# Reordered start, mLSTM stage and last stage of a one-core hybrid attention and mLSTM step

## What is computed

```python
mod = jax.nn.silu(c) @ w_ada + b_ada                       # 2048 x 6144
shift, scale, gate = jnp.split(mod[:, None, :], 3, axis=-1)
h = rmsnorm(x, norm_pre) * (1 + scale) + shift
u = h @ w_in                                               # 2048 x 13320
q_a, k_a, v_a, z_a, q_m, k_m, v_m, o_m, z_m, i_m, f_m, g_a, g_m = split_in(u)
att = attend(...)                                          # differential attention, 8 heads
y_a = (rmsnorm(att) * (1 - lam_init) * silu(z_a)) @ w_br_a
hm, C1, n1, m1 = mlstm(qm, km, vm, ig, lf, C0, n0, m0)     # 4 heads
y_m = (sigmoid(o_m) * rmsnorm(hm) * silu(z_m)) @ w_br_m
y = (sigmoid(g_a) * y_a + sigmoid(g_m) * y_m) @ w_out
out = x + gate * rmsnorm(y, norm_post)
```

## Time and profile before

| | |
|---|---|
| median of 3 runs | 1985.6 us (1985.49 to 1986.94) |
| the profiled execution | 1986.92 us, span 1985.4 us |
| TensorE busy | 1936.4 us, 98% of the span |
| VectorE, ScalarE, GpSimd busy | 781.6, 642.0, 188.5 us |
| mean granted TensorE clock | 0.995 of full |
| HBM | 220.93 MB read, 17.73 MB written, 121 GB/s mean |

### The profile page before, as it was taken

How to read it: one execution, slowest core, us unless ns; L and a number is a source line. 1 busy time by engine, 2 the same in 40 slices (tenths; PEclk the granted TensorE clock), 3 DMA queues, 4 the chain that set the end, 5 groups by cost and what they waited for, 6 DMA issues and landing times.

```text
span 1985.4 us, 31138 instructions
## 1 busy us (share of the span) xinstructions
PE 1936.4 (98%) x12223; PEld 1662.7 (84%) x12223; DVE 781.6 (39%) x1666; ACT 642.0 (32%) x1144; POOL 188.5 (9%) x316
## 2 busy tenths in 40 slices
PE   5999999999999999999999999999999999999997
PEld 4778898988899998888899988878878878878885
DVE  4555234246653334454355322232232232353224
ACT  4212222235545454343333222212222222332232
POOL 2221011000020101122230000000000000010001
PEclk9999999999999999999999999999999999999998
DMA  9986663231234542223332332232232232353223
GB/s 308 311 277 191 197 221 95 78 109 49 59 109 149 175 139 71 74 77 111 101 118 84 85 85 80 83 105 80 80 104 85 80 104 81 122 188 101 80 84 117
DMA packets 165938, 240.50 MB, mean 121 GB/s; under 512 B 15065, under 2 KB 113497, under 8 KB 164073
## 3 DMA queue, kind: packets, MB, share of 16 engines
q1 hardware_dynamic: 150304, 194.03, 31.9%
q0 software_dynamic: 13264, 44.50, 6.8%
q10 hardware_dynamic: 2242, 0.19, 0.1%
HBM read 220.93 MB, written 17.73 MB: 120 GB/s over the span
## 4 chain that ended last, share of the span: by engine, by line
PE 74%; DVE 1%; POOL 1%; issue 1%; ACT 1%; DMA 0%; ACTq 0%; POOLq 0%
PE gemm L544 59%; PE bank_s L544 9%; PE bank_o L544 2%; PE bank_a L544 2%; PE bank_s L787 1%; DVE g_m L2022 1%; PE bank_a L733 0%; PE bank_s L952 0%; PE bank_s L1064 0%; POOL hm_sq L2317 0%; POOL hm_sq L2318 0%; POOL rinv L2372 0%; ACT hm_sq L1141 0%; DVE y_tok L2102 0%; PE bank_s L573 0%
## 5 line engine op out<-in xcount | busy, mean ns | idle before, releaser
L544 PE MATMUL gemm<-h_hi,w_hi 128*128 128x288 f32 (+1 forms) x2560 | 663.0, 324 | 8.1 <-DVE q_acc L1582 4.0
L1506 DVE TENSOR_TENSOR w_lo<-w_raw,w_hi 128x512 fp32r<-128x512 f32 x512 | 357.5, 699 | 782.2 <-ACT w_hi L1141 781.6
L1141 ACT ACTIVATE w_hi<-w_raw 128x512 fp32r<-128x512 f32 x512 | 322.3, 630 | 1025.1 <-PE bank_s L544 568.7
L544 PE MATMUL gemm<-h_hi,w_lo 128*128 128x288 f32 (+1 forms) x2560 | 639.2, 315 | 0.0
L544 PE MATMUL gemm<-h_lo,w_hi 128*128 128x288 f32 (+1 forms) x2560 | 638.4, 315 | 0.0
L544 PEld LDWEIGHTS gemm<-h_hi,w_hi 128*128 128x128 f32 x2560 | 425.6, 189 | 85.9 <-issue 49.0
L544 PEld LDWEIGHTS gemm<-h_lo,w_hi 128*128 128x128 f32 x2560 | 426.0, 189 | 21.1
L544 PEld LDWEIGHTS gemm<-h_hi,w_lo 128*128 128x128 f32 x2560 | 426.3, 189 | 20.3
L544 PE MATMUL gemm<-w_hi,y_all 128*128 128x512 f32 x512 | 158.8, 391 | 0.5 <-DVE g_m L2022 0.5
L544 PEld LDWEIGHTS gemm<-w_hi,y_all 128*128 128x128 f32 x512 | 95.6, 188 | 24.9 <-DVE g_m L2022 1.4
L544 PE MATMUL gemm<-w_lo,y_all 128*128 128x512 f32 x256 | 99.9, 390 | 0.0
(11 more groups left out here) (456 smaller groups left out, 1754.2 us busy)
## 6 DMA issues: line engine op xcount, KB each, us to landing
w_raw<-in_w_in SPq DMA_DIRECT2D x384, 256.0 KB, 2.7
ada_in<-in_w_ada SPq DMA_DIRECT2D x72, 512.0 KB, 7.6
w_raw<-in_w_out SPq DMA_DIRECT2D x64, 256.0 KB, 2.4
ada_gate<-in_w_ada SPq DMA_DIRECT2D x16, 512.0 KB, 5.6
k_page<-in_cache_k POOLq DMA_DIRECT2D x16, 512.0 KB, 5.5
v_page<-in_cache_v POOLq DMA_DIRECT2D x16, 512.0 KB, 4.7
w_raw<-in_w_br_a SPq DMA_DIRECT2D x32, 256.0 KB, 2.4
w_raw<-in_w_br_m SPq DMA_DIRECT2D x32, 256.0 KB, 2.4
```

The source lines that it names most:

```text
L544: return nc.tensor.matmul(out, lhsT, rhs, start=start, stop=stop, skip_group_check=True)
L1141: return nc.scalar.activation(out, in_, func, **kw)
L1506: V.tensor_tensor(w_lo[:, slot], w_raw[:, slot], w_hi[:, slot], ALU.subtract).then_inc(lo_ready, 1)
```

## The change

Seven edits, all of them of order, engine or size of a piece:

1. TensorE runs three products of the identity with `xn_t` into `gemm[:, 0, 0, :]` behind the first row transposes; nothing reads their result. The wait for `in_wif` moves behind them.
2. In the second group, rounds 4 and 5 follow granule 0 and rounds 6 and 7 granule 1 (all four followed granule 0); the row transposes of that group go from granule 1 to granule 2, with `ss_rows` and `ss_out` one granule later on VectorE.
3. VectorE splits weights 1 and 2 behind the first h_lo, and makes the second pair's h itself (`make_h(1)`); GpSimd starts at pair 2.
4. In the later groups VectorE does the first half of `q_sum` ahead of `ss_out`.
5. mLSTM: the square of `em_b` on ScalarE goes behind the tanh of the first z block; `mls_finish(0)` goes from granule 1 of head 1 to granule 2, behind the keys and the first mask.
6. GpSimd issues the load of n0 ahead of the four loads of state C.
7. Last stage: `finish` in two halves of 1024 columns, each stored with a DMA of its own.

```diff
@@ sync, last stores
             for nth, tt in enumerate(LAST_ORDER):
-                sp.wait_ge(fin_done, nth + 1)
...
-                sp.dma_start(dst, y_tok[0:dst.shape[0], tt, :]).then_inc(stores, 16)
+                for half in range(2):
+                    sp.wait_ge(fin_done, 2 * nth + half + 1)
+                    cols = slice(half * D // 2, (half + 1) * D // 2)
+                    sp.dma_start(dst[:, cols], y_tok[0:dst.shape[0], tt, cols]).then_inc(stores, 16)
@@ tensor, q_granule
-                granule(n % RING, h_hi, h_lo, 2 * j, True, True, n if n else None, (h_lo_made, 2 * j + 2), j + 1 if v == 1 and j < KG - 1 else None)
-                if v == 0 and j < KG - 1:
+                more, rows_at = j < KG - 1, 1 if j else 2
+                granule(n % RING, h_hi, h_lo, 2 * j, True, True, n if n else None, (h_lo_made, 2 * j + 2), j + 1 if v == rows_at and more else None)
+                if j == 0 and v < 2:
+                    for k in range(AQ + 2 * v, AQ + 2 * v + 2):
+                        ada_round(k)
+                if v == 0 and j and more:
@@ tensor, ahead of the q projection
-            pe.wait_ge(in_wif, 16)
             pe.wait_ge(x_out_a, 2 * (NT + 1))
             pe.wait_ge(x_out_d, 2 * (NT + 1))
+            for kt in range(3):
+                mm(gemm[:, 0, 0, :], ident[:], xn_t[:, kt, 0:TP])
+            pe.wait_ge(in_wif, 16)
@@ scalar, granule 7 of a head
-                        act.wait_ge(mo_cp, 3 * hd + 2)
-                        go(em_b[:], em_b[:], ACT.Square, scale=math.sqrt(EPS * DV / P))
...
                             go(halves(z_act[:, cb, :]), block(cb), ACT.Tanh, scale=0.5).then_inc(z_tanh, 1)
                             if not cb:
+                                act.wait_ge(mo_cp, 3 * (d // 8) + 2)
+                                go(em_b[:], em_b[:], ACT.Square, scale=math.sqrt(EPS * DV / P))
@@ vector, first stage
             ss_rows(0)
-            for n in range(LOOKAHEAD):
-                early_lo(n)
+            early_lo(0)
             ss_out(0)
...
+            make_h(0)
             h_low(0)
+            for n in range(1, LOOKAHEAD):
+                early_lo(n)
             for n in range(QN):
                 c, v = n // 4, n % 4
                 more = c < KG - 1
                 if v == 3 and more:
                     h_low(c + 1)
-                if v == 1 and more:
-                    ss_out(c + 1)
                 early_lo(n + LOOKAHEAD)
                 if c:
-                    q_sum(c, v, n)
-                if v == 0 and more:
+                    q_sum(c, v, n, 0)
+                if v == (1 if c else 2) and more:
+                    ss_out(c + 1)
+                    if not c:
+                        make_h(1)
+                if c:
+                    q_sum(c, v, n, 1)
+                if v == (0 if c else 1) and more:
                     ss_rows(c + 1)
@@ vector, mLSTM
-                        if hd:
+                        if hd > 1:
                             mls_finish(hd - 1)
...
+                    if q == 2 and hd == 1:
+                        mls_finish(0)
@@ vector, finish
-                V.scalar_tensor_tensor(y_tok[0:n, tt, :], y_tok[0:n, tt, :], rinv[0:n, tt:tt + 1], xa, ALU.mult, ALU.add).then_inc(fin_done, 1)
+                for half in (slice(0, D // 2), slice(D // 2, D)):
+                    V.scalar_tensor_tensor(y_tok[0:n, tt, half], y_tok[0:n, tt, half], rinv[0:n, tt:tt + 1], xa[0:n, half],
+                                           ALU.mult, ALU.add).then_inc(fin_done, 1)
@@ gpsimd
-            for j in range(1, NG):
+            for j in range(2, NG):
...
                 if hd == HM - 1:
+                    pool.dma_start(n0[:], state_n[0]).then_inc(in_n0, 16)
                     state_in(0, 0)
-                    pool.dma_start(n0[:], state_n[0]).then_inc(in_n0, 16)
```

More of the change, by code:

```diff
@@ L534, in _ @@
             for nth, tt in enumerate(LAST_ORDER):
-                sp.wait_ge(fin_done, nth + 1)
                 dst = y_prompt[0, tt * P:(tt + 1) * P, :] if tt < NT else y_sample.rearrange("b t d -> (b t) d")
-                sp.dma_start(dst, y_tok[0:dst.shape[0], tt, :]).then_inc(stores, 16)
-            sp.wait_ge(stores, 16 * (NT + 1))
+                for half in range(2):
+                    sp.wait_ge(fin_done, 2 * nth + half + 1)
+                    cols = slice(half * D // 2, (half + 1) * D // 2)
+                    sp.dma_start(dst[:, cols], y_tok[0:dst.shape[0], tt, cols]).then_inc(stores, 16)
+            sp.wait_ge(stores, 32 * (NT + 1))
         @nc_block.tensor
@@ L1574, in early_lo, with q_sum @@
                 split_lo(n % RING, n)
-            def q_sum(c, v, n):
-                for cb in range(2):
-                    dve.wait_ge(*((block0_done, 4 * c + v + 1) if cb == 0 else (gemm_used, n + 1)))
-                    acc = q_acc[2 * v + cb]
-                    dst = acc[:] if c < KG - 1 else q_att[:, 2 * v + cb, :]
-                    V.scalar_tensor_tensor(halves(dst), block(cb), DH ** -0.5, halves(acc[:]), ALU.mult, ALU.add).then_inc(bank_free[cb], 1)
+            def q_sum(c, v, n, cb):
+                dve.wait_ge(*((block0_done, 4 * c + v + 1) if cb == 0 else (gemm_used, n + 1)))
+                acc = q_acc[2 * v + cb]
+                dst = acc[:] if c < KG - 1 else q_att[:, 2 * v + cb, :]
+                V.scalar_tensor_tensor(halves(dst), block(cb), DH ** -0.5, halves(acc[:]), ALU.mult, ALU.add).then_inc(bank_free[cb], 1)
             norm_x(0)
@@ L1602, in _, with make_h @@
             dve.wait_ge(x_out_d, 2 * (NT + 1))
-            dve.wait_ge(mod_done, 1)
-            for t in range(2):
-                link(V.tensor_scalar(s1[:, t, :], mod_ss[:, KT + t, :], 1.0, vec_t[:, V_PRE + t:V_PRE + t + 1], ALU.add, ALU.mult))
-            for t in range(2):
-                x3 = xn_t[:, t, TP:T].rearrange("p (b t) -> p b t", b=NB)
-                h3 = h_tmp[:, t, TP:T].rearrange("p (b t) -> p b t", b=NB)
-                V.tensor_scalar(h_tmp[:, t, 0:TP], xn_t[:, t, 0:TP], s1[:, t, 0:1], mod_ss[:, t, 0:1], ALU.mult, ALU.add)
-                link(V.tensor_tensor(h3, x3, bcast(s1[:, t, 1:9], TS), ALU.mult))
-                V.tensor_tensor(h3, h3, bcast(mod_ss[:, t, 1:9], TS), ALU.add).then_inc(h_made, 1)
+            def make_h(j):
+                dve.wait_ge(mod_done, j + 1)
+                for t in range(2):
+                    kt = 2 * j + t
+                    link(V.tensor_scalar(s1[:, t, :], mod_ss[:, KT + kt, :], 1.0, vec_t[:, V_PRE + kt:V_PRE + kt + 1], ALU.add, ALU.mult))
+                if j:
+                    dve.wait_ge(gates_mm, j)
+                    dve.wait_ge(h_hi_made, 2 * j)
+                    dve.wait_ge(h_lo_made, 2 * j)
+                for t in range(2):
+                    kt = 2 * j + t
+                    x3 = xn_t[:, kt, TP:T].rearrange("p (b t) -> p b t", b=NB)
+                    h3 = h_tmp[:, t, TP:T].rearrange("p (b t) -> p b t", b=NB)
+                    V.tensor_scalar(h_tmp[:, t, 0:TP], xn_t[:, kt, 0:TP], s1[:, t, 0:1], mod_ss[:, kt, 0:1], ALU.mult, ALU.add)
+                    link(V.tensor_tensor(h3, x3, bcast(s1[:, t, 1:9], TS), ALU.mult))
+                    V.tensor_tensor(h3, h3, bcast(mod_ss[:, kt, 1:9], TS), ALU.add).then_inc(h_made, 1)
+            make_h(0)
             h_low(0)
+            for n in range(1, LOOKAHEAD):
+                early_lo(n)
             for n in range(QN):
```

## The result

The changed kernel took 1976.29 us (median of 6 runs, 1975.15 to 1976.71) against 1985.55 (1985.28 to 1987.11) for the kernel before on the same chip: ratio 0.995, 95% interval 0.9937 to 0.9963, 9.3 us faster. The forecast was 1974.7, range 1971.3 to 1978.2. The profiled executions stand at 1986.92 and 1976.41, 10.5 apart.

A forecast was written before the change was run, and what follows sets the result against it. TensorE, busy 98% of the span, was taken as the bound, so only its stops and low clock counted. 0 + 4.0 + 1.1 + 1.8 + 3.2 + 0.8 = 10.9 us off the profiled 1986.92; median forecast 1974.7, range 1971.3 to 1978.2.

The forecast's parts named there:

- The start: First groups through round 11: granule 0 ends 3.8 us earlier, counted as zero; bounds 3.8 gained, 1.0 lost.
- Net 0.0: Start: granule 4 may start 0.9 later, the wait at round 11; it starts near 59.8, so nothing is gained or lost.
- The string of loads: SyncE's queue: round 11's load stands behind weight 7, which waits for weight 3's split; it holds round 11 until 66.58, unchanged.
- three signs of being wrong: Round 11 over 0.5 from 66.6; clock 0.5 between 42 and 1960; wait over 0.3 per head at mls_squares.
- The q sums: Granule 5 and its five counterparts: TensorE's six stops for q additions go, 4.0 us gained, bounds 3.4 to 4.0.
- The weighed keys: mLSTM heads: without mls_finish(0) in front, VectorE weighs the keys sooner; 1.1 us gained, bounds 0.6 to 1.1.
- The last granules: Last granule of each head: tanh uses ScalarE's idle time before em_b's square; 1.8 us gained, ends 0 and 2.5.
- the third rival: Waits move instead of going: q term halves, head term is 0, gain 7.1, so 1978.5 us; chance 10%.
- n0: Sample states: load issued 2.87 earlier, stop of 1.7 and low-clock loss of 1.5 go; 3.2 us gained, bounds 1.7 and 3.2.
- The rival that light products make the clock fall: Sample states: light products before n0, not the stop, lower the clock; only 1.7 of 3.2 goes, 1976.2 us; chance 14%.
- The last stage: Halved finish and store: 0.8 us gained, middle of 1.2 and 0.4; the latter charges 0.8 for VectorE's handover to GpSimd.
- The slower rival: First groups: TensorE's stops keep the clock low for a whole group, costing 12.8 us, so 1987.5; chance 3%.

The follow-up runs named there:

- start_as_before: Changed kernel with its new start (three identity products, second group's order, VectorE's splits and second h) taken back: 1975.33 us, ratio 0.9944 to the kernel before.
- clock_fill: Changed kernel plus unread TensorE products, two of 512 columns ahead of the second pair's gates and one of 128 behind: 1974.92 us, ratio 0.9943.
- h_ahead_of_split: Changed kernel with ss_out(1) and make_h(1) on VectorE ahead of the split of weight 5 instead of behind it: 1974.91 us, ratio 0.9942.
- h_and_loads_ahead: Changed kernel with ss_out(1) and make_h(1) ahead of weight 5's split, and SyncE issuing rounds 8 to 11 ahead of weight 7: 1973.32 us, ratio 0.9935.
- combined: Changed kernel with second pair's h chain and loads of rounds 8, 9 earlier, ScalarE's em_b square last, halved finish for two tiles only: 1971.48 us, ratio 0.9924.
- q_sums_only: Kernel before with only the first half of q_sum moved ahead of ss_out in the later groups: 1980.37 us against 1985.78, ratio 0.997.
- keys_only: Kernel before with only mls_finish(0) moved: 1984.91 us against 1985.78, ratio 0.9993.
- em_only: Kernel before with only the square of em_b moved behind the first tanh: 1985.72 us against 1985.78, ratio 0.9999.
- em_square_last: Changed kernel with ScalarE's order first tanh, square of hm, second tanh, square of em_b; GpSimd waits for the latter only before its second sum: 1974.53 us.
- n0_only: Kernel before with only n0's load issued first: 1983.05 us against 1986.37, ratio 0.9986.
- no_dummies: Changed kernel without the three identity products ahead of the first gates: 1976.44 us, ratio 0.9953 to the kernel before.

## Why the prediction was right, and where it was not

The sum of 10.9 met 10.5 between the profiled executions, and part of that is luck: the start and the last granules gave 2.0 less than forecast, the q sums and the keys 1.6 more. The median moved by 9.3, less than the trace. The sizes of four of the six terms were off.

- **The start, counted at zero, cost 0.87 in the trace and 1.0 to 1.5 in the medians (start_as_before).** The step that failed is "Net 0.0": that TensorE's stops before granule 4 would eat no more than the spare. The stops came as forecast (1.86 for 2.0), granule 4 started at 60.02 for 59.8, but at the clock of 0.50. That was the bound of 1.0 lost, which I had set aside. clock_fill shows the cause, and h_ahead_of_split, h_and_loads_ahead and combined, which have no stop there either, also keep the clock at 1.00 from 60 to 63. The string of loads that was to hold round 11 did not bind in the changed kernel, whose TensorE came later than the load. It does bind once h is early: h_ahead_of_split is held until 66.36, and h_and_loads_ahead, with another order on SyncE, isn't. The prediction took that string as given from a stretch of full engines; the gap ahead of it was worth 1.6 in the median.
- **Its own signs.** Two of the three signs of being wrong came: round 11 started near 67.5 (an estimate, three rounds of 0.89 behind 64.88) instead of 66.6, and the clock was 0.50 from 60 to 63. The longer wait for round 11's load did not come, and granule 0 was over at 42.08, not by 41.5. The time lay in the range all the same, since the start is only one term of six.
- **The q sums: 4.0 forecast, 5.30 measured**, in the changed kernel as in q_sums_only. All six stops went. The term was priced by the list of waits, 0.68 each; each stop cost 0.88 on the timeline. What the 0.2 consist of was not tried by itself; the product behind a stop is also longer, 0.50 against 0.42.
- **The weighed keys: 1.1 forecast, 1.40 measured** (keys_only). The same size error.
- **The last granules: 1.8 forecast, 0.63 measured** (em_only). "I take 1.8, nearer to the upper one, as VectorE's and GpSimd's parts all follow ScalarE" failed: I let the first tanh move up and did not ask for the second one, which now stood behind both squares (em_square_last moves one square back and gets 0.85 more). The 0.63 and the keys' 1.40 make up the 2.06 of the table. The waits moved, as the third rival has it, but here alone; its q part is refuted.
- **n0: 3.2 forecast, 3.18 in the trace** (1.73 and 1.45), 3.3 in the median of n0_only. The rival that light products make the clock fall is refuted: with the transposes and without the stop the clock stays 1.00 behind them in all ten traces that have edit 6, and with both it fell in the traces of the kernel before and q_sums_only and not in those of keys_only and em_only.
- **The last stage: 0.8 forecast, 0.76 measured**, partly for other reasons. The last landing fell from 3.9 to 2.9, by 1.0 and not 1.5, and VectorE's last finish ended 9.63 behind TensorE's last product instead of 9.48. The last four halves took 4.86 where two whole instructions took 4.69. Of the 0.8 that the handover to GpSimd was to cost the forecast took half, and none of it came: GpSimd's power took 1.52 instead of 2.59, and VectorE's second half did not wait for it. VectorE and GpSimd of the changed kernel:

```profile
1966.70 4.86 DVE L2126 SCALAR_TENSOR_TENSOR y_tok<-y_tok,rinv,x_again 128x1024 f32<-128x1024 f32 x4
```

```profile
1966.86 1.52 POOL L2397 TENSOR_TENSOR rinv<-rinv,neg_half 128x1 f32<-128x1 f32 x1 [1.72 <-DVE rinv L2119]
```

- **The median.** From a profile 1.3 above the median I took the whole 10.9. Part of that 1.3 is the low clock behind n0, present in the profiled execution: the six runs of before fall into four at 1985.3 to 1985.6 and two at 1986.9 and 1987.1. That these are the executions without and with it is inferred from the 1.5 between them, not seen, and other runs speak against so clean a split: the 47 runs of the kernel before in the other groups fill the space from 1984.3 to 1987.7 with no gap of that size, and n0_only, without that stop, still has two runs of eleven 1.3 and 1.7 above its median. The slower rival did not come: the clock fell for most of one granule in both traces.

## What to carry to other kernels

Price a stop of TensorE by the distance of the products around it, not by its entry in the list of waits, and look after the change for short delays that the list leaves out. When an engine's instruction is moved up, follow the last of the instructions behind it as well as the first. Before calling a string of loads fixed, look at the DMA share slice by slice for a gap, also ahead of the full stretch, and ask what the load behind the gap waits for in the queue. A stop that can't be avoided is worth filling with products that nobody reads: they cost no time here and made the full clock likelier. In the start, where 1.2 to 1.8 of the stop were left behind them, the clock stayed in six traces of seven. In clock_fill, where 0.16 and 0.18 were left, it stayed in its one trace, and the five runs spread over 0.3 (the changed kernel's over 1.6 and 0.8).

## What the runs showed of the hardware

**The clock behind a stop is not the same in each execution.** Behind n0's stop (1.48 to 1.67) the granted clock fell in two traces (0.50 from 897 to 900 in the kernel before, 0.57 from 890 to 893 in q_sums_only) and stayed 1.00 in two. Behind the stops of 1.86 and 0.60 ahead of granule 4 it fell in both traces of the changed kernel and not in em_square_last and no_dummies. Those two are also the ones whose granule 0 had run at the low clock, so that what TensorE did earlier could matter; no run separates that from chance. The Trainium skill, TensorE: Matmul & The Clock Gate, "Part 1: The HAM clock gate", says that the monitor behind the clock runs freely and does not start anew with the kernel, so the same work meets it at different points; the traces agree with that rule, though none tests it. One profile is not enough to price such a stop.

**GpSimd's sum and VectorE's instruction on two SBUF inputs wait for each other.** The first sum took 1.30 in the changed kernel and 1.78 in em_square_last. In both VectorE was multiplying `att`, for another 0.11 (767.40 + 0.76 - 768.05) and 0.62 (766.44 + 0.76 - 766.58): 1.19 and 1.16 are left. In the kernel before it is 1.79 less 0.64 (772.29 + 0.76 - 772.41), 1.15. VectorE in em_square_last:

```profile
766.44 0.76 DVE L1941 SCALAR_TENSOR_TENSOR att<-z_act,att 128x576 f32<-128x576 f32 x1
```

The Trainium skill, SBUF — State Buffer, "SBUF: two separate sides", has this as an exclusive lock for a whole instruction, and these three sums and the power of the last stage agree. The other direction shows behind GpSimd's second sum. In the changed kernel that sum ends at 769.43 + 1.81 = 771.24, and VectorE's split takes 1.78 where 0.69 is usual and ends 0.55 later:

```profile
770.01 1.78 DVE L1514 TENSOR_TENSOR w_lo<-w_raw,w_hi 128x512 fp32r<-128x512 f32 x1
```

The kernel before and em_square_last have the same 0.55 and 0.54. At the power on one column, between two halves of `finish`, no such wait of VectorE shows (2.46 for the pair). With the multiplication of `att` behind GpSimd's first sum em_square_last might gain the other 0.3 a head that was expected; that was not tried.

**The landing of the same load differs.** In the traces of the six kernels with the old start round 11 waited for its load in four (0.34 to 0.90) and started there between 65.55 and 66.58; in the other two it did not wait. TensorE's first product behind it lay between 66.50 and 67.58. A bound by loads that is read from one trace is good to about 1.
